# RWKV block: the exclusive cumulative log decay computed by a VectorE subtraction instead of a third masked product on TensorE

## The reference, cut to what matters

```python
w_log = -softplus(-(w0 + tanh(xw @ w1) @ w2)) - 0.5
decay = exp(-exp(w_log))
def step(s, inp):
    r_t, w_t, k_t, v_t, kk_t, a_t = inp
    sa = einsum('bhij,bhj->bhi', s, -kk_t)
    s = s * w_t[:, :, None, :] + sa[..., None] * (kk_t * a_t)[:, :, None, :] + v_t[..., None] * k_t[:, :, None, :]
    return s, einsum('bhij,bhj->bhi', s, r_t)
```

## Time and profile before

| what | value |
|---|---|
| median of three runs | 2222.6 us (2220.37 to 2223.26) |
| the profiled execution: its own time | 2221.23 us |
| its span, first to last instruction | 2219.4 us |
| mean granted TensorE clock | 0.964 |
| TensorE matmul busy | 92% of the span |
| VectorE busy | 48% |
| ScalarE busy | 31% |

### The profile page before, as it was taken

How to read it: one execution, slowest core, us unless ns; L and a number is a source line. 1 busy time by engine, 2 the same in 40 slices (tenths; PEclk the granted TensorE clock), 3 DMA queues, 4 the chain that set the end, 5 groups by cost and what they waited for, 6 DMA issues and landing times. The chain is left out here.

```text
span 2219.4 us, 55745 instructions
## 1 busy us (share of the span) xinstructions
PE 2049.8 (92%) x24578; PEld 1330.7 (60%) x24578; DVE 1076.1 (48%) x2577; ACT 682.0 (31%) x1853; POOL 226.4 (10%) x225
## 2 busy tenths in 40 slices
PE   8999978997999999999989999789979999999997
PEld 4665667775566566754456656577754665667543
DVE  2016047674566457833320160477745664588333
ACT  1122044443455442310012220444434554423100
POOL 0000000001000024301100000000010000243022
PEclk9999989997999989999999999899979999899999
DMA  5102010000000337732111020100000003377221
GB/s 199 48 1 85 0 40 4 4 4 22 2 1 1 86 149 277 266 124 71 63 59 48 1 85 1 40 4 4 4 23 1 1 1 86 152 282 258 87 78 57
DMA packets 49843, 150.85 MB, mean 68 GB/s; under 512 B 15106, under 2 KB 19458, under 8 KB 40132
## 3 DMA queue, kind: packets, MB, share of 16 engines
q1 hardware_dynamic: 37316, 71.79, 9.7%
q0 software_dynamic: 12288, 75.51, 9.2%
HBM read 129.70 MB, written 12.86 MB: 64 GB/s over the span
## 5 line engine op out<-in xcount | busy, mean ns | idle before, releaser
L373 PE MATMUL psum<-work 128*128 128x368 f32 (+1 forms) x1632 | 515.3, 477 | 8.9 <-DMA work<-w_z 6.6
L373 PEld LDWEIGHTS psum<-work 128*128 128x128 f32 (+1 forms) x1632 | 308.1, 189 | 212.7 <-issue 26.7
L2191 PE MATMUL psum<-work,mixed 128*128 128x512 f32 (+1 forms) x576 | 252.9, 600 | 1.6 <-PEq L1863 1.6
L2191 PEld LDWEIGHTS psum<-work,mixed 128*128 128x128 f32 (+1 forms) x576 | 107.8, 188 | 140.3 <-issue 140.3
L2059 DVE STREAM_TRANSPOSE work<-work 128x1024 f32<-128x1024 f32 x128 | 150.5, 1214 | 0.4 <-issue 0.3
L1635 ACT ACTIVATE work<-psum,work 128x128 f32<-128x128 f32 (+8 forms) x130 | 97.9, 753 | 160.5 <-DVE work L1738 160.0
L1519 PE MATMUL psum<-work 96*128 96x512 f32 (+3 forms) x384 | 139.6, 498 | 3.7 <-ACT work L1635 2.1
L1803 POOL DMA_INDIRECT work<-cache_ckv,pages x64 | 60.7, 948 | 623.4 <-PE psum L1469 386.4
L1963 PE MATMUL psum<-work,ckv 128*64 128x256 f32 x1024 | 118.0, 382 | 0.7 <-ACT ckv L2018 0.7
L1519 PEld LDWEIGHTS psum<-work 96*128 96x128 f32 x384 | 68.4, 193 | 62.4 <-issue 45.8
L2239 DVE SCALAR_TENSOR_TENSOR work<-work,psum 128x512 f32<-128x512 f32 (+1 forms) x36 | 23.1, 683 | 166.2 <-PE psum L2191 166.2
(11 more groups left out here) (260 smaller groups left out, 3130.5 us busy)
## 6 DMA issues: line engine op xcount, KB each, us to landing
work<-w_z SPq DMA_DIRECT2D x4, 2560.0 KB, 11.3
work<-w_out SPq DMA_DIRECT2D x4, 2048.0 KB, 9.0
xres<-work SPq DMA_DIRECT2D x16, 512.0 KB, 2.9
work<-xT SPq DMA_DIRECT2D x4, 1104.0 KB, 8.9
work<-x_tok SPq DMA_DIRECT2D x8, 512.0 KB, 3.9
work<-xres SPq DMA_DIRECT2D x8, 512.0 KB, 4.2
work<-w_z SPq DMA_DIRECT2D x1, 2304.0 KB, 12.7
o_ckv<-ckv SPq DMA_DIRECT2D x2, 1104.0 KB, 4.3
```

Source lines behind the costliest of these rows:

```text
L373: return nc.tensor.matmul(zb[i % 2][n][rows, 0:G], z_weights(m, g)[:, k, lo:lo + Z_W[i]], xT[:, k, span(n)], start=k == 0, stop=k == DK - 1)
L2191: last = nc.tensor.matmul(yb[t % 2][half][0:n, :], m.mixed[:, k, lo:lo + n], wo[half][:, k, :], start=k == 0, stop=k == DK - 1)
```

## The change

The product with C_MS is dropped; C_GT keeps its place in bank 3. VectorE gets a function for `sums`: it waits for `s_cum`, subtracts `logd` from the inclusive sums in bank 2, writes the difference into `dec[:, 2]` in SBUF and raises a new semaphore, `s_strict`. ScalarE takes the exponential of `dec[3]` first, waits for `s_strict`, then takes `dec[2]` (in place), `dec[0]` and `dec[1]`. On VectorE the new instruction stands where `sums` stands in the list: behind `write` (L1253) and ahead of `finish` (L1277), and in the front between `decay` (L1137) and `keys_norm` (L1141).

```diff
+    s_strict = sem("s_strict")
 # TensorE, sums
-                for i, c in enumerate((C_MI, C_MS, C_GT)):
-                    nc.tensor.matmul(bank[2 + i // 2][:, (i % 2) * WA:(i % 2 + 1) * WA], sqc(c), logd,
+                for i, c in enumerate((C_MI, C_GT)):
+                    nc.tensor.matmul(bank[2 + i][:, 0:WA], sqc(c), logd,
                                      start=True, stop=True)
 # ScalarE, sums
-                for i, (src, sign) in enumerate(((bank[2][:, 0:WA], -1.0), (bank[2][:, 0:WA], 1.0),
-                                                 (bank[2][:, WA:2 * WA], -1.0), (bank[3][:, 0:WA], -1.0))):
+                nc.scalar.activation(dec[:, 3, :], bank[3][:, 0:WA], ACT.Exp, scale=-LOGD)
+                act.wait_ge(s_strict, t + 1)
+                for i, src, sign in ((2, dec[:, 2, :], -1.0), (0, bank[2][:, 0:WA], -1.0), (1, bank[2][:, 0:WA], 1.0)):
                     nc.scalar.activation(dec[:, i, :], src, ACT.Exp, scale=sign * LOGD)
 # VectorE
+            def sums(t, _):
+                dve.wait_ge(s_cum, t + 1)
+                nc.vector.tensor_tensor(dec[:, 2], bank[2][:, 0:WA], logd, ALU.subtract).then_inc(s_strict, 1)
-            run({"mix": mix, "decay": decay, ...
+            run({"mix": mix, "sums": sums, "decay": decay, ...
```

More of the change, by code:

```diff
@@ L1309, in _ @@
             nc.vector.tensor_copy(gnb, bank[4][:, 0:2 * P:P])
-            run({"mix": mix, "decay": decay, "keys_norm": keys_norm, "unit": unit, "keys_decay": keys_decay,
+            run({"mix": mix, "sums": sums, "decay": decay, "keys_norm": keys_norm, "unit": unit, "keys_decay": keys_decay,
                  "bonus": bonus_, "prod": prod, "n2": squares, "z1": z1, "z2": z2, "z3": z3, "zf": zf, "read": read,
```

## The result

The changed kernel takes 2249.7 us, the median of four runs (2237.7 to 2254.7), against 2222.9 us before: a ratio of 1.0108, 95% interval 1.0061 to 1.0154. The forecast was 2225 us with a range of 2221 to 2230. The change is slower, by some 27 us in the medians (24 by the ratio, which is one of means), where +2.5 was forecast. The four runs rise as their mean granted clock falls: 2237.7 us at 0.949, 2248.0 at 0.944, 2251.5 at 0.942, 2254.7 at 0.941; before it was 0.964. The profiled execution is the first of them, +16.5 us against that of before, so its rows show only a part of the effect.

The account below looks back on a forecast made before the run. TensorE and VectorE were taken to bound each iteration by halves, handing over at add L1201. Terms +3.5 - 1.9 + 0.9 = +2.5 us on 2222.6 gave 2225 us; 8-in-10 range 2221 to 2230.

Parts of the forecast that it names:

- What sets the period: RWKV loop: the start of VectorE's add L1201 of `z3`; its gain or loss passes one for one to the next iteration.
- without a gap: VectorE from the add L1201 to L1187 in iteration 3: 24 rows without an idle entry, 377.62 to 388.44.
- The dropped product, 0.467 us: TensorE's L806: one product of two matmuls less per `sums`, so what follows on TensorE can start 0.467 us earlier.
- Iterations 2 to 9, 0.22 us each: Loop, both layers: L1201 starts 0.22 us later behind subtraction and `finish`; sixteen iterations, +3.5 us, between +2.4 and +8.0.
- Iterations 0 and 1, -0.467 us each: Loop iterations without `finish`: the subtraction ends inside a wait, L1201 comes 0.467 us earlier; four iterations, -1.9 us.
- The front: Ahead of the loop: the subtraction delays L1141, L1143 and L1162; both fronts +0.9 us, between 0.7 and 1.2.
- ScalarE: In the loop: the reordered exponentials cost nothing, ending near 378.2 against 378.4 before, with cover of some 0.8 us.
- The sum without the clock: Whole kernel: +3.5 - 1.9 + 0.9 = +2.5 us, between +1.2 and +7.3.
- rival C: Iterations 2 to 8: the longer wait at `mid` lets TensorE's clock fall; +34 us at most, 2259 us; chance 2%.
- +34 us: Most that a fallen clock could cost: 2.4 us in each of the 14 iterations 2 to 8.
- the 0.93 us wait: TensorE at `mid`: its wait for VectorE's L1195 grows from 0.24 to 0.93 us.

Follow-up runs that it names:

- experiment 3: The kernel after with two spare products (256 and 192 columns) on TensorE ahead of `mid` in iterations 2 to 9: 2227.9 us, ratio 1.0000.
- experiment 7: The kernel after with one spare product of 256 columns on TensorE ahead of `mid` in iterations 2 to 9: 2230.8 us, ratio 1.0029.
- Experiment 8: The kernel before without the C_MS product and with no subtraction; the exclusive exponential is taken of the inclusive sums: 2224.2 us, ratio 0.9999.
- experiments 9 and 10: Kernel after with `finish` and `keys_norm` ahead of sums (9), kernel before (10), both with spare products in iterations 0, 1, 9 and front: 2212.1, 2222.1 us.
- experiment 2: The kernel after with the product by C_MS put back ahead of the sums of chunks, its result unused: 2250.7 us, ratio 1.0104.
- experiment 6: The kernel after with the sums and subtraction moved into `z3` behind `keys_norm`, ScalarE's exponentials into `mid`: 2225.4 us, ratio 0.9999.

## Why the prediction was wrong

- **What sets the period**: right. From the add of `z3` to L1193 (L1187 before) runs the chain; moving `finish` out of it brings the period to 0.42 us below that of before, and more work on TensorE (experiments 3, 7) leaves it alone. But "without a gap" holds only at full clock: in iteration 3 of the kernel after VectorE waits 0.72 us for TensorE inside it.
- **The dropped product, 0.467 us**: right. Experiment 8 shortens the shortest iterations by 0.44 us (21.58 against 22.02).
- **Iterations 2 to 9, 0.22 us each**: right. The add is 0.18 us late and the period 0.21 longer. By the Trainium skill's rule on emptying the pipe ("VectorE: DVE Perf Modes", Terms, DRAIN) the add would have been an estimated 0.33 us late; the rows, 0.34 us from the subtraction to an instruction that doesn't need it, speak against the rule here.
- **Iterations 0 and 1, -0.467 us each**: right on VectorE (in iteration 0, L811 to the add took 1.03 us after and 1.04 before), but their time together did not fall: they run partly at the low clock in both kernels, and experiments 9 and 10 show 0.43 us in both, where it is held at 1.00.
- **The front**: right in its chain (2.95 us against 2.88), late by another 0.34 us by the clock.
- **ScalarE**: right. The last exponential and the small fifth are done by 379.5 in iteration 3, and the copy that TensorE waits for comes at 380.34.
- **The sum without the clock**: experiment 3, the kernel after with the clock held in iterations 2 to 9, is level with before, -0.2% to +0.2%; +2.5 us lies in that, as would no change at all; its mean of iterations 2 to 8, 0.20 us above before, says more.
- **The step that failed** is the chance of rival C, 2%, with its reason "The waits would still be apart from each other". They are apart, and the clock fell all the same, in 10 of 14 iterations. The sum therefore holds no term for the clock in iterations 2 to 8. The prediction had the mechanism, its sign and a size (+34 us) and even forecast the 0.93 us wait; it had only iterations 0 and 3 to go by, which stand on either side of the case and don't place it, and took the favourable one. Its +34 us "at most" is also mis-sized: a mean of 0.75 between levels of 0.5 and 1.00 means half of the time at the lower one, not a quarter, which makes 4.8 us an iteration and 68 in all. Measured, a fallen iteration lost 1.06 us (23.29 against 22.23). By the ratios the change costs 24 us; with the waits filled it costs nothing (experiment 3) or 6 us (experiment 7), which leaves some 18 to 24 us for the clock. In the profiled pair 5.7 us of it lie in iterations 2 to 8 (a mean of 22.99 against 22.58 in experiment 3, 14 times) and 2.7 in iteration 9 of the first layer (20.70 against 18.00); the rest of the 18 to 24 us no trace places.

What stays open: why ten iterations fall and four with the same waits don't, and where the slower executions, of which there is no trace, lose another 10 to 17 us. Iterations at full clock scatter between 22.02 and 22.90 us already before: in the six longest (22.47 and more) TensorE stands still once for 0.23 to 0.54 us, 8 to 10 us into the iteration, with no wait that the profile shows; in the other eight (22.26 at most) it does not. What holds it there is open. The stretches between the two loops and behind the second take 892 to 900 and 592 to 600 us in the twelve profiled executions, so the total of one execution says little about a few microseconds.

## What to carry to other kernels

Taking work from an engine that then waits can cost more than the work: read the granted clock by stretch before forecasting a gain from TensorE, and treat each new wait of TensorE as a price. Spare products put into such a wait cost the chain nothing and held the clock here; with them, and with the subtraction behind `finish`, a change that had lost 24 us gave 10. A new VectorE instruction that waits belongs behind the ready ones, not ahead of them.

## What the runs showed of the hardware

- With a wait of 0.87 or 0.88 us at `mid`, in a kernel with TensorE busy 92%, 22 of 28 iterations 2 to 8 fell to the lower level for a part of their 22 us (kernel after, experiment 2); with 0.25 us or less there, 3 of 140 (the ten other kernels). The length of the wait alone does not decide: 0.75 us ahead of the product of `z3` left seven iterations of experiment 6 at 1.00. In a fallen stretch 32 products of L844 take 0.65 instead of 0.45 us, and those of L898 1.9 instead of 1.08. The Trainium skill ("TensorE: Matmul & The Clock Gate", Part 1) says that the default is the throttled level and that activity releases it; iteration 3 of the kernel after agrees, with a clock that falls behind the wait and is back at full speed while TensorE works.
- Removed work can do it too: experiment 8 has nearly the waits of before in iteration 9 (0.86 against 0.84 us at `mid`) and falls to 0.78 and 0.79 in the two layers, where before was at 1.00 in both.
- A VectorE subtraction of 128 x 256 that reads PSUM takes 0.42 or 0.43 us, and the next independent one starts 0.34 us after it.
